# Second feed forward of a two-block transformer: three pairs of gate and up chunks as seven block products, weight blocks summed by accumulating DMA

## The chip, the cores and the metric

The kernel is one program on one core of one Trainium2 chip. The metric is device microseconds (us) of one execution. TensorE is called PE, VectorE DVE, ScalarE ACT, GpSimd POOL and SyncE SP, as in the profile.

## What is computed

The reference runs two transformer blocks on 256 tokens of width 1024, the second on the output of the first, all in float32. What matters here is the end of the second block, its gated feed forward, with a hidden width of 2816:

```python
x = x + merged @ w_out[layer]
h = rmsnorm(x, norm_ffn[layer])
x = x + (jax.nn.silu(h @ w_gate[layer]) * (h @ w_up[layer])) @ w_down[layer]
return rmsnorm(x, norm_final)
```

`w_gate` and `w_up` are 1024 x 2816, `w_down` is 2816 x 1024.

## The kernel before

Each product keeps float32 accuracy by splitting both operands in a high half, which the PE's reduced float32 format holds, and a low rest: x is held as `AH` and `AL`, a weight block as `WH` and `WL`, and a product is three matmuls, high x high, high x low and low x high (`part`, lines 441, 442 and 443). The stationary operand is a 128 x 128 block of the activation, the moving one up to 512 columns of the weights, and the result accumulates in a bank of PSUM, 128 tokens by 512 columns.

**The ring of weights.** `weight_units` lists all weight blocks in the order of use, as units of 1 MB, 128 partitions by 2048 floats. In the feed forward they go round six slots of SBUF (2, 3, 0, 1, 4, 5). `W32` of a slot receives the load; `WL` of the same slot overwrites it in place, and `WH` has its own memory. SP issues the loads in this order (`load`, line 316) and before each waits until PE is done with the unit that had the slot before; so a unit is loaded at the earliest when the sixth unit before it has been used up. ACT then writes `WH`, a copy in the reduced format, in two halves (`hi()`, line 1071), and DVE writes `WL` = `W32` - `WH`, in two halves (`lo()`, line 1579). Each engine's program is an order written out by hand, and each engine takes its instructions strictly in that order.

**The feed forward.** The hidden width is cut in 11 chunks of 256. A chunk c has two units of gate and up columns (256 and 256 columns side by side, four k tiles each) and one unit of `w_down` (two k tiles by 1024). `up2(c, tb)` multiplies one block of 128 tokens (tb is 0 or 1) by both units: 24 matmuls of 512 columns into bank 4 + tb, gate in the left half, up in the right. ACT takes silu of the gate half (`silu_gate`, line 1511), DVE multiplies it by the up half (`gated`) into `hid`, PE turns `hid` with transposes against the identity into bank 6 or 7 (`hid_turn`, line 758; the banks alternate, and a bank is free again when DVE has written the low half `HL` from it), ACT and DVE split what was turned in `HH` and `HL`, and `down2(c, tb)` multiplies by the down unit into banks 0 to 3, which hold the sum over all chunks. On PE a middle chunk is: `up2(c, 0)`, `up2(c, 1)`, `down2(c - 1, 0)`, `down2(c - 1, 1)`, and the two turns of chunk c. That is 48 + 24 matmuls of 512 columns and 4 transposes. On DVE it is `lo()`, `gated`, `lo()`, `gated`, `lo()` and two `HL`.

Besides its small reciprocal square roots (line 343) POOL has nothing to do in this part.

## Time and profile before

| | us |
|---|---|
| median of 3 runs (lowest to highest) | 726.88 (726.67 to 726.91) |
| the profiled execution | 726.56 |
| its span, first to last instruction | 724.7 |
| PE, DVE, ACT, POOL busy in the span | 715.0, 516.7, 410.6, 25.9 |

The profiled execution took 1.9 us more than its span; the median of the three runs is 0.3 us above it. In rows of the trace, "x" is a count; "idle before" is the time in which an engine had nothing to run, with what ended it; PE's own matmul time overlaps (a matmul is shown for 0.39 us where the next one starts after 0.23), so that starts, not durations, tell its rate. PEclk is the granted clock of TensorE as a share of full speed, the DMA share is the mean busy share of the core's 16 DMA engines.

### The profile page before, as it was taken

How to read it: one execution, taken by the hardware profiler on the slowest of the kernel's cores; microseconds unless marked ns; L12 is line 12 of the kernel's file. 1: busy time of each engine (PE TensorE's matmuls, PEld its weight loads, DVE VectorE, ACT ScalarE, POOL GpSimd, SP SyncE). 2: the span in 40 equal slices, each digit the busy share in tenths (PEclk: the TensorE clock that was granted, in tenths of full speed). 3: DMA queues.
4: the chain of work that ended last, by engine and by line, in shares of the span. 5: the costliest groups of instructions: out<-in, count | busy, mean ns of one | idle time of the engine just before them, and what ended most of it. 6: DMA issues, size and time to landing. Idle time of an engine off the chain costs nothing.

```text
span 724.7 us, 9660 instructions
## 1 busy us (share of the span) xinstructions
PE 715.0 (99%) x3746; PEld 572.5 (79%) x3746; DVE 516.7 (71%) x911; ACT 410.6 (57%) x691; POOL 25.9 (4%) x43
## 2 busy tenths in 40 slices
PE   8999999999999999999999999999999999999996
PEld 4678885588888888888888777778888888888885
DVE  4789999898666867847898799766856555455544
ACT  3487658985845564456556676675465443344432
POOL 1030012001000000000100000000000000000000
PEclk9999999999999999999999999999999999999999
DMA  9996939517656576643558334443366556555511
GB/s 363 415 370 229 387 104 356 204 59 261 225 180 230 203 264 242 224 175 115 162 202 291 117 119 148 151 165 121 115 229 232 178 196 202 179 175 175 175 58 59
DMA packets 72989, 145.94 MB, mean 201 GB/s; under 512 B 4128, under 2 KB 27680, under 8 KB 71920
## 3 DMA queue, kind: packets, MB, share of 16 engines
q1 hardware_dynamic: 71136, 140.03, 55.1%
q0 software_dynamic: 1520, 5.03, 2.0%
q8 instruction: 30, 0.49, 0.3%
q10 hardware_dynamic: 288, 0.27, 0.1%
q14 instruction: 15, 0.12, 0.0%
HBM read 144.27 MB, written 1.05 MB: 201 GB/s over the span
## 4 chain that ended last, share of the span: by engine, by line
PE 95%; issue 2%; DVE 1%; ACT 1%; POOL 0%; POOLq 0%; DVEq 0%
PE bank L441 23%; PE bank L443 23%; PE bank L442 23%; PE bank L786 5%; PE bank L423 5%; PE bank L784 3%; PE bank L460 1%; PE bank L515 1%; PE bank L523 1%; PE bank L518 1%; PE bank L918 1%; PE bank L940 1%; PE bank L624 1%; PE bank L500 1%; PE bank L646 1%
## 5 line engine op out<-in xcount | busy, mean ns | idle before, releaser
L1579 DVE TENSOR_TENSOR WL<-W,WH 128x1024 fp32r<-128x1024 f32 (+2 forms) x222 | 249.7, 1169 | 35.4 <-ACT WH L1071 35.3
L1071 ACT ACTIVATE WH<-W 128x1024 fp32r<-128x1024 f32 (+2 forms) x222 | 211.9, 1011 | 49.7 <-DMA W<-in_w_mlp 35.8
L441 PE MATMUL bank<-WH,AHL 128*128 128x512 f32 (+1 forms) x480 | 188.8, 393 | 0.0
L443 PE MATMUL bank<-WH,AHL 128*128 128x512 f32 (+1 forms) x480 | 185.3, 386 | 0.0
L442 PE MATMUL bank<-WL,AHL 128*128 128x512 f32 (+1 forms) x480 | 185.2, 386 | 0.0
L441 PEld LDWEIGHTS bank<-WH,AHL 128*128 128x128 f32 x480 | 90.2, 188 | 20.4 <-issue 3.2
L443 PEld LDWEIGHTS bank<-WH,AHL 128*128 128x128 f32 x480 | 90.2, 188 | 18.7
L442 PEld LDWEIGHTS bank<-WL,AHL 128*128 128x128 f32 x480 | 90.3, 188 | 17.0
L441 PE MATMUL bank<-WH,HH 128*128 128x512 f32 (+1 forms) x218 | 84.9, 390 | 0.0
L443 PE MATMUL bank<-WH,HL 128*128 128x512 f32 (+1 forms) x218 | 84.5, 388 | 0.0
L442 PE MATMUL bank<-WL,HH 128*128 128x512 f32 (+1 forms) x218 | 84.4, 387 | 0.0
L786 PE MATMUL bank<-AHL,WH 128*128 128x512 f32 x168 | 60.5, 398 | 0.0
L784 PE MATMUL bank<-AHL,WL 128*128 128x256 f32 x192 | 50.0, 281 | 0.0
L443 PEld LDWEIGHTS bank<-WH,HL 128*128 128x128 f32 x218 | 40.9, 188 | 8.5
L442 PEld LDWEIGHTS bank<-WL,HH 128*128 128x128 f32 x218 | 41.0, 188 | 8.3
L441 PEld LDWEIGHTS bank<-WH,HH 128*128 128x128 f32 x218 | 40.9, 188 | 8.0
L1511 ACT ACTIVATE rel<-bank 128x256 f32<-128x256 f32 x22 | 8.5, 384 | 62.2 <-PE bank L443 61.1
L1588 DVE TENSOR_TENSOR hid<-bank,rel 128x256 f32<-128x256 f32 x22 | 9.3, 424 | 42.2 <-ACT rel L1511 42.2
L784 PEld LDWEIGHTS bank<-AHL,WL 128*128 128x128 f32 x192 | 36.3, 189 | 2.0
L786 PEld LDWEIGHTS bank<-AHL,WH 128*128 128x128 f32 x168 | 31.6, 188 | 6.7
L1594 DVE SCALAR_TENSOR_TENSOR cacc<-hp,vec,cacc 128x256 f32<-128x256 f32 x88 | 36.0, 478 | 0.2
L1914 DVE TENSOR_TENSOR HL<-bank,HH 128x256 fp32r<-128x256 f32 (+1 forms) x26 | 11.1, 461 | 30.9 <-ACT HH L1079 30.9
(287 smaller groups left out, 852.1 us busy)
## 6 DMA issues: line engine op xcount, KB each, us to landing
W<-in_w_mlp SPq DMA_DIRECT2D x32, 1024.0 KB, 5.4
W<-in_w_in SPq DMA_DIRECT2D x24, 1024.0 KB, 5.0
W<-in_w_gate SPq DMA_DIRECT2D x22, 512.0 KB, 4.0
W<-in_w_up SPq DMA_DIRECT2D x22, 512.0 KB, 5.2
W<-in_w_down SPq DMA_DIRECT2D x11, 1024.0 KB, 4.9
W<-in_w_ada SPq DMA_DIRECT2D x10, 1024.0 KB, 8.6
WX<-in_w_ada SPq DMA_DIRECT2D x10, 1024.0 KB, 10.4
W<-in_w_out SPq DMA_DIRECT2D x8, 1024.0 KB, 5.3
```

Of the source, the lines that this page charges most:

```text
L423: ins = e.transpose(bank[b][:, c * 128:c * 128 + 128], src, m.ident[:, :])
L441: e.matmul(po, hs, wh[:, k, c0:c0 + cw], start=first and k == 0, stop=False)
L442: e.matmul(po, hs, wl[:, k, c0:c0 + cw], start=False, stop=False)
L443: ins = e.matmul(po, ls, wh[:, k, c0:c0 + cw], start=False, stop=last and k == unit.nk - 1)
L784: ins = e.matmul(bank[4 + j][:, 0:256], wl[:, k, js], m.AH[:, 4 * i + k, :], start=False, stop=False)
L786: ins = e.matmul(both, wh[:, k, js], m.AHL[:, :, 4 * i + k, :], start=False, stop=i == 1 and k == 3)
L1071: e.activation(m.WH[unit.slot][:, c], m.W32[unit.slot][:, c], ACT.Copy).then_inc(S["w_hi"], 1)
L1511: e.activation(m.rel[tb][:, 0:256], bank[bk][:, 0:256], ACT.Silu).then_inc(S["silu_g"], 1)
L1579: e.tensor_tensor(m.WL[unit.slot][:, c], m.W32[unit.slot][:, c], m.WH[unit.slot][:, c].bitcast(F32), ALU.subtract).then_inc(S["w_lo"], 1)
L1588: e.tensor_tensor(o, a, b, op).then_inc(S[sem], 1)
L1594: e.scalar_tensor_tensor(o, a, scalar, b, op0, op1).then_inc(S[sem], 1)
L1914: e.tensor_tensor(L[:, k0:k0 + nj, ts], bank[b][:, 0:nj * 128].rearrange("p (j n) -> p j n", j=nj), H[:, k0:k0 + nj, ts].bitcast(F32), ALU ...
```

## The change

Chunks 3 and 4, 5 and 6, and 7 and 8 become three groups (`PAIRS`, `GROUPS`); chunks 0, 1, 2, 9 and 10 stay as they were. The groups are numbered 0 to 7, and the pairs are groups 3, 4 and 5. For a pair, let G0, G1 be the lower and upper half of the rows of its 512 gate columns, U0, U1 those of its 512 up columns, A00, A01 the lower and upper half of the features of token block 0, and A10, A11 those of block 1. Eight products of a 128 x 512 by a 512 x 512 block would give gate and up of both token blocks. The change makes seven, each 12 matmuls (`quad_sum` and `part`):

```
0: (A10 - A11) G0            bank 4     1: (A01 - A00) U1            bank 5
2: (A00 - A11) (G0 - U1)     bank 6     3: A11 (G0 + G1)     onto bank 4
4: A00 (U0 + U1)     onto bank 5        5: (A01 - A11) (G1 + U1)     onto bank 4
6: (A10 - A00) (G0 + U0)     onto bank 5
```

Bank 4 after product 3 is the gate of block 1, bank 5 after product 4 the up of block 0; with `ysum` = product 0 + product 1 - product 2, the gate of block 0 is bank 4 + `ysum` after product 5, and the up of block 1 is bank 5 + `ysum` after product 6.

The five differences of activations (`FS`, `FH`, `FL`) are made once, ahead of chunk 2. The weights of a product are one unit of 1 MB. Those of products 0 and 1 are loaded. That of product 2 is the difference of these two, formed by DVE (`difference`, two instructions of 1024 columns) into a seventh slot. Those of products 3 to 6 are loaded by SP, and then POOL waits for that load and issues a second one of 1 MB from the other block, with `accum_op=ALU.add` (line 452 of the changed kernel), which adds to what lies in the slot; `hi()` of the unit waits for this second load. The seventh unit does not take part in the ring of six. The two down units of a pair are used together by `down2` of the pair, and a turn of a pair has four transposes instead of two. PE starts products 0 and 1 of the next group (`begin`) ahead of the pair's turns. A few semaphores are merged and renamed with no other effect.

```diff
+        self.W32.append(M("W32_6", 76, [128, 2048]))
+        self.WL.append(M("WL_6", 76, [128, 2048], F32R))
+        self.WH.append(M("WH_6", 8, [128, 2048], F32R))
...
+        self.FL = [M(f"FL{i}", (70, 72, 74, 0, 2)[i], [128, 4, 128], F32R) for i in range(5)]
+        self.ysum = M("ysum", 4, [128, 512])
+        self.g0 = M("g0", 6, [128, 512])
+        self.u0, self.u1 = self.g1b[:, 0:512], self.g1b[:, 512:1024]
...
+GROUPS = [(c, c in PAIRS) for c in range(11) if c - 1 not in PAIRS]
+NG = len(GROUPS)
+GU_ORDER = [(0, 0), (1, 0), (0, 1), (1, 1)] + [(g, tb) for g in range(2, NG) for tb in range(2)]
+HID_AT = {gt: i + 1 for i, gt in enumerate(GU_ORDER)}
...
+DN_ORDER = [(g, tb) for g in range(NG - 2) for tb in range(2)] + [(NG - 2, 0), (NG - 1, 0), (NG - 2, 1), (NG - 1, 1)]
...
+    def quad_unit(g, n, src, i, plus=None):
+        c0 = 256 * GROUPS[g][0]
+        add(("gu", g), src, 4 * i, 4, [(src, c0, 512)], True, ("gu_mm", QUAD_AT[g] + n + 1))
+        if plus:
+            w, j = plus
+            units[-1].plus = d[w][512 * j:512 * j + 512, c0:c0 + 512].rearrange("(k p) n -> p k n", p=128)
...
+    for g in range(NG + 1):
+        if g < NG and GROUPS[g][1]:
+            quad_unit(g, 0, "w_gate_2", 0)
+            quad_unit(g, 1, "w_up_2", 1)
+            first, second = units[-2:]
+            units.append(Unit(4, 512, [], True, (S["gu_mm"], QUAD_AT[g] + 3)))
+            units[-1].difference = (first, second)
+            by["gu", g].append(units[-1])
+            quad_unit(g, 3, "w_gate_2", 1, ("w_gate_2", 0))
+            down_units(g - 1)
+            quad_unit(g, 4, "w_up_2", 0, ("w_up_2", 1))
+            quad_unit(g, 5, "w_gate_2", 1, ("w_up_2", 1))
+            quad_unit(g, 6, "w_gate_2", 0, ("w_up_2", 0))
+            continue
...
-    while len(slots) < len(units):
-        slots.append((2, 3, 0, 1, 4, 5)[(len(slots) - 38) % 6])
+    ring = itertools.cycle((2, 3, 0, 1, 4, 5))
+    for unit in units[38:]:
+        slots.append(6 if unit.difference else next(ring))
...
+        if unit.plus is not None:
+            unit.base = unit.landed
+            n = sum(1 for other in units[:units.index(unit)] if other.plus is not None)
+            unit.landing_plus = S[f"l_s{n % 4}"]
+            unit.landed = (unit.landing_plus, 32 + 16 * (n // 4 + 1))
...
+    for unit in units:
+        if unit.plus is not None:
+            w.wait_ge(unit.base[0], unit.base[1])
+            e.dma_start(unit.block(m), unit.plus, accum_op=ALU.add).then_inc(unit.landing_plus, 16)
...
+    def hid_turn2(g, tb):
+        if GROUPS[g][1]:
+            turns["n"] = 1
+        hid_turn(g, 4 if GROUPS[g][1] else 2, tb, ("hid2", HID_AT[g, tb], 16 + 2 * g + tb + 1))
...
+    def begin(g):
+        if GROUPS[g][1]:
+            quad_sum(g, 0, 0, 4, True)
+            quad_sum(g, 1, 1, 5, True)
+        else:
+            up2(g, 0)
...
+    def rest(g):
...
+        quad_sum(g, 2, 2, 6, True)
+        frees(6, ("quad", 4 * q + 2))
+        w.wait_ge(S["quad_act"], 2 * q + 1)
+        part(by["gu", g][3], m.AH, m.AL, 4, 1, 4, False, True, "gu_mm", n_ready(2, 1), onto=True)
+        for tb in range(2):
+            down2(g - 1, tb, False, False)
+        w.wait_ge(S["quad"], 4 * q + 1)
+        part(by["gu", g][4], m.AH, m.AL, 0, 0, 5, False, True, "gu_mm", n_ready(2, 0), onto=True)
+        w.wait_ge(S["silu"], SILU_AT[g, 1])
+        quad_sum(g, 5, 3, 4, False)
+        frees(4, ("quad", 4 * q + 3))
+        w.wait_ge(S["quad_act"], 2 * q + 2)
+        quad_sum(g, 6, 4, 5, False)
+        frees(5, ("quad", 4 * q + 4))
 
     up2(0, 0)
...
+        rest(g)
+        if GROUPS[g][1]:
+            begin(g + 1)
+            hid_turn2(g, 0)
+            hid_turn2(g, 1)
+        else:
+            hid_turn2(g, 0)
+            hid_turn2(g, 1)
+            if g < NG - 2:
+                begin(g + 1)
+    up2(NG - 1, 0)
...
+    def quad_group(g):
+        q = quads.index(g)
+        lo(1 + GROUPS[g - 1][1])
+        w.wait_ge(S["gu_mm"], QUAD_AT[g] + 2)
+        w.wait_ge(S["quad_act"], 2 * q + 1)
+        tt(m.ysum[:, :], bank[5][:, :], m.ysum[:, :], ALU.add, "quad")
+        w.wait_ge(S["gu_mm"], QUAD_AT[g] + 3)
+        w.wait_ge(S["quad"], 4 * q + 1)
+        tt(m.ysum[:, :], bank[6][:, :], m.ysum[:, :], ALU.subtract, "quad")
+        lo(3)
+        if GROUPS[g + 1][1]:
+            difference(g + 1)
+        lo()
+        w.wait_ge(S["gu_mm"], QUAD_AT[g] + 6)
+        w.wait_ge(S["quad"], 4 * q + 2)
+        if q:
+            w.wait_ge(S["silu"], SILU_AT[quads[q - 1], 0])
+        tt(m.g0[:, :], bank[4][:, :], m.ysum[:, :], ALU.add, "quad")
+        lo()
+        w.wait_ge(S["gu_mm"], QUAD_AT[g] + 7)
+        tt(m.u1, bank[5][:, :], m.ysum[:, :], ALU.add, "quad")
+        w.wait_ge(S["hid_turned"], 4 + 2 * (g - 2) + 2)
+        w.wait_ge(S["silu"], SILU_AT[g, 0])
+        w.wait_ge(S["quad_act"], 2 * q + 2)
+        tt(m.hid[g % 2][:, 0, :], m.u0, m.rel[0][:, :], ALU.mult, "hid2")
+        w.wait_ge(S["quad"], 4 * q + 4)
+        tt(m.hid[g % 2][:, 1, :], m.u1, m.rel[1][:, :], ALU.mult, "hid2")
+        lo(2)
 
     norm_features(5, 1, m.ffn, None)
     gated(0, 0)
...
```

Where a group's turns stand on PE: the end of a chunk's down product, the turns of both token blocks, and the next chunk's first product, before. `HH0`, `HL0` are the turned hidden values of an even chunk, `hid1` those to be turned.

```order
L441 MATMUL bank3<-WH_4_65,HH0_166 128x512
L442 MATMUL bank3<-WL_4_59,HH0_166 128x512
L443 MATMUL bank3<-WH_4_65,HL0_168 128x512
L423 MATMUL bank7<-ident_80,hid1_165 128x128 x2
L423 MATMUL bank6<-ident_80,hid1_165 128x128 x2
L441 MATMUL bank4<-WH_5_66,AHL_96 128x512
L442 MATMUL bank4<-WL_5_60,AHL_96 128x512
L443 MATMUL bank4<-WH_5_66,AHL_96 128x512
```

The same place on PE now, the end of product 1 of the second pair, the turns of the first pair, and product 2 of the second pair:

```order
L505 MATMUL bank5<-WH_4_65,FH1_213 128x512
L506 MATMUL bank5<-WL_4_59,FH1_213 128x512
L507 MATMUL bank5<-WH_4_65,FL1_223 128x512
L487 MATMUL bank7<-ident_80,hid1_165 128x128 x8
L505 MATMUL bank6<-WH_6_211,FH2_214 128x512
L506 MATMUL bank6<-WL_6_210,FH2_214 128x512
L507 MATMUL bank6<-WH_6_211,FL2_224 128x512
```

The turns of the two token blocks used banks 7 and 6; both now use bank 7 (bank 6 is taken by product 2), and so the second one follows the `HL` instruction that reads the first.

On DVE, one chunk before, from the first `gated` of an odd chunk to its `HL`:

```order
L1588 TENSOR_TENSOR hid1_165<-bank4,rel0_170 128x256
L1579 TENSOR_TENSOR WL_2_57<-W32_2_51,WH_2_63 128x1024 x2
L1588 TENSOR_TENSOR hid1_165<-bank5,rel1_171 128x256
L1579 TENSOR_TENSOR WL_3_58<-W32_3_52,WH_3_64 128x1024 x2
L1914 TENSOR_TENSOR HL1_169<-bank7,HH1_167 128x2x128
L1914 TENSOR_TENSOR HL1_169<-bank6,HH1_167 128x2x128
```

On DVE now, from the difference for the second pair to the `HL` of the first pair:

```order
L1726 TENSOR_TENSOR W32_6_209<-W32_1_50,W32_4_53 128x1024 x2
L1717 TENSOR_TENSOR WL_1_56<-W32_1_50,WH_1_62 128x1024 x2
L1726 TENSOR_TENSOR g0_228<-bank4,ysum_227 128x512
L1717 TENSOR_TENSOR WL_4_59<-W32_4_53,WH_4_65 128x1024 x2
L1726 TENSOR_TENSOR g1b_74<-bank5,ysum_227 128x512
L1726 TENSOR_TENSOR hid1_165<-g1b_74,rel0_170 128x512
L1726 TENSOR_TENSOR hid1_165<-g1b_74,rel1_171 128x512
L1717 TENSOR_TENSOR WL_6_210<-W32_6_209,WH_6_211 128x1024 x2
L1717 TENSOR_TENSOR WL_5_60<-W32_5_54,WH_5_66 128x1024 x2
L2052 TENSOR_TENSOR HL1_169<-bank7,HH1_167 128x4x128 x2
```

Between the last multiplication into `hid` and the `HL` stood one weight unit, and now there stand two, the second of them (slot 5) a unit that an accumulating load completes.

## Rows read from the trace of the kernel before

**Rows 1.** The page: span, busy shares, granted clock, chain that ended last.

```profile
span 724.7 us, 9660 instructions
PE 715.0 (99%) x3746; PEld 572.5 (79%) x3746; DVE 516.7 (71%) x911; ACT 410.6 (57%) x691; POOL 25.9 (4%) x43
PEclk9999999999999999999999999999999999999999
PE 95%; issue 2%; DVE 1%; ACT 1%; POOL 0%; POOLq 0%; DVEq 0%
```

**Rows 2.** Windows: one chunk, the feed forward's middle, the end; columns in the first line.

```profile
core 0: us, PE busy (x) PEld busy (x) DVE busy (x) ACT busy (x) POOL busy (x), PEclk, DMA share, GB/s
603.79:620.59 16.80, 16.80 (x77) 13.91 (x77) 8.70 (x11) 7.11 (x10) 0.00 (x0) 1.00 0.58 187
540.00:700.00 160.00, 160.00 (x730) 132.40 (x729) 87.93 (x104) 71.82 (x104) 0.00 (x0) 1.00 0.54 178
700.00:725.00 25.00, 18.79 (x91) 15.51 (x89) 8.75 (x19) 5.34 (x15) 1.08 (x2) 0.94 0.12 43
```

**Rows 3.** Timeline of PE in one chunk: start us, length us.

```profile
602.92 0.39 PE L441 MATMUL bank<-WH,AHL 128*128 128x512 f32 x1
...
604.28 0.39 PE L441 MATMUL bank<-WH,AHL 128*128 128x512 f32 x1
...
611.77 0.60 PE L423 MATMUL bank<-ident,hid 128*128 128x128 f32 x4
612.12 0.48 PE L441 MATMUL bank<-WH,AHL 128*128 128x512 f32 x1
```

**Rows 4.** Timeline of the issues of SP's loads over one chunk.

```profile
603.79 0.37 SPq L316 DMA_DIRECT2D W<-in_w_gate  x1
...
606.51 0.37 SPq L316 DMA_DIRECT2D W<-in_w_gate  x1
...
611.96 0.37 SPq L316 DMA_DIRECT2D W<-in_w_down  x1
620.59 0.37 SPq L316 DMA_DIRECT2D W<-in_w_gate  x1
```

**Rows 5.** Windows with the DMA engines full: 2 KB, 1 KB and 4 KB rows.

```profile
231.00:235.00 4.00, 4.00 (x25) 3.51 (x24) 0.11 (x1) 1.20 (x2) 0.00 (x0) 1.00 1.04 395
606.50:611.00 4.50, 4.50 (x21) 3.72 (x21) 2.79 (x3) 2.28 (x3) 0.00 (x0) 1.00 1.08 360
614.00:616.00 2.00, 2.00 (x10) 1.65 (x10) 2.00 (x2) 0.80 (x1) 0.00 (x0) 1.00 1.02 422
```

**Rows 6.** DMA issues by line: size of each, median us from issue to landing.

```profile
W<-in_w_mlp SPq DMA_DIRECT2D x32, 1024.0 KB, 5.4
...
W<-in_w_down SPq DMA_DIRECT2D x11, 1024.0 KB, 4.9
...
g1b<-in_final_g POOLq DMA_DIRECT2D x1, 512.0 KB, 4.3
```

**Rows 7.** Groups by form of the last 185 us: busy us, mean ns, idle before.

```profile
L1579 DVE TENSOR_TENSOR WL<-W,WH 128x1024 fp32r<-128x1024 f32 x60 | 70.7, 1222 | 14.0 <-ACT WH L1071 14.0
L1071 ACT ACTIVATE WH<-W 128x1024 fp32r<-128x1024 f32 x58 | 58.1, 1054 | 0.1
L1588 DVE TENSOR_TENSOR X<-bank,X 128x512 f32<-128x512 f32 x4 | 2.8, 692 | 3.7 <-PE bank L443 3.7
L1083 ACT ACTIVATE S<-X 128x512 f32<-128x512 f32 x3 | 1.9, 632 | 6.7 <-DVE X L1588 6.7
```

**Rows 8.** Timeline of DVE and ACT: a weight unit's two halves back to back.

```profile
607.89 2.36 DVE L1579 TENSOR_TENSOR WL<-W,WH 128x1024 fp32r<-128x1024 f32 x2 [0.52 <-ACT WH L1071]
606.80 2.00 ACT L1071 ACTIVATE WH<-W 128x1024 fp32r<-128x1024 f32 x2
```

More of the change, by code:

```diff
@@ L187, in __init__ @@
         self.nk, self.wid, self.pieces, self.split, self.free = nk, wid, pieces, split, free
+        self.plus = self.difference = None
     def block(self, m):
@@ L288, in weight_units @@
             last[p] = unit
+        if unit.difference:
+            unit.landed = (S["diff"], 2 * sum(1 for other in units[:units.index(unit) + 1] if other.difference))
+            continue
         landed[slot] = landed.get(slot, 0) + 16 * len(unit.pieces)
@@ L311, in load @@
         unit = units[n]
+        if unit.difference:
+            return
         for old in unit.old:
@@ L425, in turn, with part @@
         return b
-    def part(unit, H, L, k0, tb, bk, first, last, sem, ready, c0=0, cw=512):
+    def part(unit, H, L, k0, tb, bk, first, last, sem, ready, c0=0, cw=512, onto=False):
         wh = m.WH[unit.slot][:, 0:unit.nk * unit.wid].rearrange("p (k n) -> p k n", k=unit.nk)
@@ L440, in part @@
             ls = L[:, k0 + k, tb * 128:tb * 128 + 128]
-            e.matmul(po, hs, wh[:, k, c0:c0 + cw], start=first and k == 0, stop=False)
-            e.matmul(po, hs, wl[:, k, c0:c0 + cw], start=False, stop=False)
-            ins = e.matmul(po, ls, wh[:, k, c0:c0 + cw], start=False, stop=last and k == unit.nk - 1)
+            e.matmul(po, hs, wh[:, k, c0:c0 + cw], start=first and k == 0, stop=False, skip_group_check=onto)
+            e.matmul(po, hs, wl[:, k, c0:c0 + cw], start=False, stop=False, skip_group_check=onto)
+            ins = e.matmul(po, ls, wh[:, k, c0:c0 + cw], start=False, stop=last and k == unit.nk - 1, skip_group_check=onto)
         ins.then_inc(S[sem], 1)
@@ L1018, in down2 @@
+    def down2(g, tb, first, last, ns=(0, 1)):
         for n in ns:
-            unit = by["dn", c][0]
-            part(unit, m.HH[c % 2], m.HL[c % 2], 0, tb, 2 * n + tb, first, last, "dn_mm",
-                 lambda k: ("hid_lo", 16 + 2 * c + tb + 1), 512 * n, 512)
+            for i, unit in enumerate(by["dn", g]):
+                part(unit, m.HH[g % 2], m.HL[g % 2], 2 * i, tb, 2 * n + tb, first and i == 0, last, "dn_mm",
+                     lambda k: ("hid_lo", 16 + 2 * g + tb + 1), 512 * n, 512)
@@ L1112, in scalar_program @@
     w.wait_ge(S["l_cs"], 16)
-    e.activation(m.cs[:, :], m.cs[:, :], ACT.Silu).then_inc(S["silu_c"], 1)
+    e.activation(m.cs[:, :], m.cs[:, :], ACT.Silu).then_inc(S["silu"], 1)
     for tb in range(2):
@@ L1530, in scalar_program @@
         hid_hi2(1, tb)
-    for c in range(2, 10):
-        hi()
-        silu_gate(c, 0)
-        hi()
-        silu_gate(c, 1)
-        hi()
+    for i in range(5):
+        form_hi(i)
+    for g in range(2, NG - 1):
+        if GROUPS[g][1]:
+            quad_group(g)
+        else:
+            hi()
+            silu_gate(g, 0)
+            hi()
+            silu_gate(g, 1)
+            hi(2 if GROUPS[g + 1][1] else 1)
         for tb in range(2):
-            hid_hi2(c, tb)
+            hid_hi2(g, tb)
     hi()
-    silu_gate(10, 0)
-    hid_hi2(10, 0)
+    silu_gate(NG - 1, 0)
+    hid_hi2(NG - 1, 0)
     def last_squares(tb):
@@ L2272, in vector_program, with gated @@
     lo()
-    def gated(c, tb, bk=None):
+    quads = [g for g in range(NG) if GROUPS[g][1]]
+    def gated(g, tb, bk=None):
         bk = 4 + tb if bk is None else bk
-        w.wait_ge(S["silu_g"], GU_AT[c, tb] // 2)
-        if c > 1:
-            w.wait_ge(S["hid_turned"], 4 + 2 * (c - 2) + tb + 1)
-        tt(m.hid[c % 2][:, tb, 0:256], bank[bk][:, 256:512], m.rel[tb][:, 0:256], ALU.mult, "hid2")
-    def hid_lo2(c, tb):
-        hid_lo(c, 2, tb, 16 + 2 * c + tb + 1)
+        w.wait_ge(S["silu"], SILU_AT[g, tb])
+        if g > 1:
+            w.wait_ge(S["hid_turned"], 4 + 2 * (g - 2) + tb + 1)
+        tt(m.hid[g % 2][:, tb, 0:256], bank[bk][:, 256:512], m.rel[tb][:, 0:256], ALU.mult, "hid2")
@@ new lines, in difference, with quad_group @@
+    def difference(g):
+        unit = by["gu", g][2]
+        for old in unit.old:
+            w.wait_ge(old.free[0], old.free[1])
+        for source in unit.difference:
+            w.wait_ge(source.landed[0], source.landed[1])
+        for p in range(2):
+            c = slice(1024 * p, 1024 * p + 1024)
+            x, y = (m.W32[source.slot][:, c] for source in unit.difference)
+            tt(m.W32[unit.slot][:, c], x, y, ALU.subtract, "diff")
+    def quad_group(g):
+        q = quads.index(g)
+        lo(1 + GROUPS[g - 1][1])
[11 more added lines that the diff above has]
+        w.wait_ge(S["quad"], 4 * q + 2)
+        if q:
+            w.wait_ge(S["silu"], SILU_AT[quads[q - 1], 0])
[10 more added lines that the diff above has]
+        lo(2)
```

225 lines of the change are left out of this document (140 added, 85 removed).

## Prediction

> **What bounds the kernel now.** I read the page first [rows 1]: PE is busy 715.0 of 724.7 us, the chain that ended last is 95% PE, and the granted clock is full in every slice. Then the windows [rows 2]: in one chunk of the feed forward PE is busy 16.80 of 16.80 us, while DVE works 8.70, ACT 7.11, and the DMA engines are busy 58% of the time; from 540 to 700 us the picture is the same. So PE alone sets the time here and only fewer matmuls shorten it, but each of the three others has a known distance to PE, and the change moves all three. The timeline of PE gives the unit of account [rows 3]: from 602.92 to 604.28 six matmuls started, 0.227 us each. 72 of them are 16.3 us of the chunk's 16.80 (the period of the issues in [rows 4]); the other 0.5 us is the four transposes.
>
> **What PE saves.** Seven products of 12 matmuls replace eight: 12 fewer per pair, 36 in all, which is also what the two programs' rows differ by (2490 against 2526 of 512 columns; the transposes stay the same in number). 36 x 0.227 = 8.2 us. The Trainium skill (TensorE: Matmul & The Clock Gate, "Wait — 56ns, not 53.3ns?") gives 215.7 ns as the start to start time of 512 columns; by it the gain would be 7.8 us. The trace's 227 ns is what I use. A pair then needs 84 + 48 matmuls and 8 transposes: 132 x 0.227 + 1.0 = 30.9 us of PE, where two chunks needed 33.6.
>
> **What DVE and ACT get.** A weight unit costs DVE 2.36 us and ACT 2.00 us [rows 8] (each half 1.22 and 1.05 us by itself, [rows 7]). Two chunks have 6 units, a pair in the middle has 7 + 2 = 9. DVE: 9 x 2.36 = 21.2, the difference of two units 2.4 (the same shape), and eight instructions of 512 columns (two into `ysum`, g0, u1, two `hid`, two `HL`) at 0.69 [rows 7], 5.5: together 29.1 us against 17.4 before (2 x 8.70, [rows 2]). That is 94% of PE's 30.9. ACT: 9 x 2.00 + six of 0.63 = 21.8 us. Totals fit, so neither costs anything by its sum; what costs is DVE's order. The forming of the five activation differences (5 + 5 instructions of 0.69 us on DVE, 5 of 0.63 on ACT, before chunk 2) lies in chunks where DVE has 8.1 us free of 16.8 [rows 2], and what follows it on DVE, the `HL` of chunk 1, isn't wanted by PE until 48 matmuls later; nothing.
>
> **The wait that the turns add.** Both turns of a pair use bank 7, and the second may start only when DVE's `HL` has read the first. After PE's product 6 DVE has u1, two `hid` (3 x 0.69), two weight units (4.7) and `HL` (0.69): 7.5 us, plus 0.3 us by which DVE comes late, since between the ends of products 5 and 6 (2.7 us) stand g0 and a unit (3.05 us). PE has in that time 24 matmuls of the next group and the first four transposes, 5.4 + 0.5 = 5.9 us. PE waits about 2 us in each pair, three times: 6 us. Everything behind the second turn on PE waits too, product 2 and 3 of the next group and the down product. The bounds are 3 us (DVE never late) and 11 us (DVE late by a unit and a half, as the difference ahead of it makes possible). This alone takes most of the 8.2 us.
>
> **What the DMA engines get.** Before, a chunk loads 3 MB in 16.8 us. With the engines full, the trace shows 395 GB/s for rows of 2 KB and 422 for rows of 4 KB [rows 5], so 2.65 us for a gate or up unit of a pair (its rows are 2 KB) and 2.5 for a down unit. A pair in the middle needs six loads of 2 KB rows and two down units, 20.9 us, and four accumulating loads of 1 MB. The trace has no accumulating load. Its lower bound is the plain load, 2.65 us: the same bytes come from memory. It can't be below that. But an addition into the slot has to fetch what lies there as well: two MB read for one written. If reading is what fills an engine, it takes 5.3 us. I take 5.3, since nothing in the kernel shows an engine reading faster than it writes, and 2.65 as the other end; nothing in the trace bounds it above.
>
> Then the sum over the three pairs. Let T0 be the start of product 0 of the first pair. By the ring of six, the units of products 0, 1, 3 and 4 have been requested before T0 (the last of these 5.9 us before, when chunk 2's second unit is used up: 606.51 against the period's 603.79 and 620.59 in [rows 4] gives the place), that of product 5 is requested 0.9 us before, that of 6 at T0 + 2.7. So at T0 there are left 18 plain loads (2 of this pair, 8 of each of the next two, four of them down units) and 11 accumulating ones. PE needs the last one at the start of product 6 of the last pair: 25.4 (first pair, with one down unit) + 30.9 + 27.2 (six products and the down products) = 83.5 us after T0, and the load has to be down some 3 us before (landing, one half by ACT, one by DVE), 80.4. DMA work: 14 x 2.65 + 4 x 2.5 + 11 x 2.65 = 76 us at the lower end, which just fits; at 5.3 it is 47 + 58 = 105 us, 25 us too much. Loads hardly run ahead of that, since SP may fill a slot only when PE is done with the sixth unit before it: **the ring holds no stock for the DMA engines to work off.**
>
> To this comes time in which the engines stand idle although they are the bound. A load takes 5.4 us to land where 1 MB is 2.65 us of work, and a POOL load of half that size 4.3 us [rows 6]: about 3 us of each are not transfer. An accumulating load begins only when POOL has seen the first one landed, 12 times; most of these 36 us lie beside other loads. I charge a sixth, 6 us; the bounds are 0 and 12. The Trainium skill (DMA: Bandwidth & Descriptors, "Issuing engines are not separate DMA queues") says that loads issued from different engines run on the same 16 DMA engines; by that rule POOL's loads bring no bandwidth of their own, and the sum above would stand.
>
> **The sum.** 25 (DMA) + 6 (idle) + 2 (turn wait of the last pair, where no load can hide it; in the others the DMA wait covers it) - 8.2 = +25 us. The profiled execution took 726.6, so 751.5; from the median 726.9 it is 751.9. I predict 752. Its own range is 740 (an accumulating load at 4.3 us) to 765 (12 us idle and PE at a lower clock after its longest waits: at the end of the kernel, where PE idles 6.2 of 25 us, the granted clock is 0.94 [rows 2], that is 3 us at half speed).
>
> **The rivals.**
> (a) An accumulating load costs no more than a plain one. The DMA work then fits (76 of 80 us), PE waits for the turns and, in the first pair, for a chain of load, addition and split that is too long (0 to 6, I take 3). Of the turns I take 9 here rather than 6, since nothing but DVE's queue then sets them and in two pairs the difference (2.4 us) stands in it ahead of g0: 9 + 3 - 8.2 = +4, so 731, from 725 (turns 6, chain 0) to 736 (11 and 6). For it: the bytes from memory are the same. The Trainium skill (same page, "Where 436 GB/s comes from") puts the ceiling at 435 GB/s; at that rate 29 MB would take 70 us, and by it this rival would stand; the trace's full windows show 360 to 422 [rows 5].
> (b) The other side, faster: the additions are hidden as in (a), and DVE's queue runs far enough ahead that the second turn finds bank 7 free. It decides at one point: whether `HL` of the first turn comes within 5.9 us of product 6's end. By instruction counts it comes after 7.5; two units of 2.36 us would have to be done earlier, which their place in DVE's order excludes unless product 6 itself is late. Then 36 matmuls less 1 or 2 us of waits: 720, from 718 to 725.
> (c) An accumulating load costs far more than two plain ones, 8 us: 47 + 88 = 135 us, 55 too much, and PE at the lower clock between: about 782.
> (d) The change doesn't do what it says. The programs' rows exclude it: 36 matmuls are gone.
>
> **How the numbers follow.** Forecast 0.5, (a) 0.28, (b) 0.08, (c) 0.12, the rest 0.02. The range is to hold 8 in 10: from 728, inside (a), to 772, which leaves out (b), the lowest part of (a) and (c). Within 0.2% (1.45 us, about what a measurement of this kernel can tell from no change) lies only a strip of (a): 0.05. Faster: (b) and a little of (a), 0.09. Slower 0.86.
>
> **What would show it.** In the profile after: 36 fewer matmuls of 512 columns; the start to start time still 0.227 us. In the windows of the pairs, the DMA share near 1 for some 80 to 110 us where it was 0.55, and PE busy well below its window; the first weight halves on ACT (`WH`) waiting for a DMA, DVE for ACT, PE for `WL`. The landing of POOL's accumulating loads: 8 us or more from issue supports 5.3 us of work, 5 to 6 us supports (a). PE idle about 2 us before a transpose of line 487, released by `HL`, in all three pairs. It would be wrong if the DMA share stays below 0.9 and the landings short (then (a)), or if no transpose waits (then the step on DVE's order fails), or if ACT never waits for a load in the pairs.

## The result, and the profile after

The changed kernel takes 757.5 us (median of 4 runs, 754.6 to 759.1) where the kernel before took 726.8 (4 runs, 726.6 to 726.9): 1.0418 times as long, 95% interval 1.0381 to 1.0456, or 30.7 us more. The profiled execution took 754.6 us, 28.0 more than that of before.

The page of the changed kernel, the lines that answer to [rows 1], and that on the DMA engines:

```profile
span 752.6 us, 9651 instructions
PE 715.1 (95%) x3710; PEld 569.6 (76%) x3710; DVE 554.5 (74%) x945; ACT 433.4 (58%) x708; POOL 41.3 (5%) x55
...
PEclk9999999999999999999999999999999979989999
DMA  8995949424675676465384334433578999999611
```

PE has 36 matmuls fewer and is busy just as long (715.0 before). Both can hold only if the remaining ones ran more slowly, and the clock line says where: at the end of the kernel, in the slices where the DMA line stands at 9. (The page's chain that ended last covers only 17% of the span here, so the readings below go by windows and timelines.)

Windows of the changed kernel: from the issue of product 3's unit to the third pair, from the start of product 0 of the first pair to the start of product 6 of the last (answers to the second line of [rows 2]), and one stretch in which PE worked at the lower clock:

```profile
core 0: us, PE busy (x) PEld busy (x) DVE busy (x) ACT busy (x) POOL busy (x), PEclk, DMA share, GB/s
561.71:690.00 128.29, 104.37 (x432) 83.11 (x431) 82.35 (x88) 60.71 (x75) 15.32 (x12) 0.92 1.04 278
578.68:695.45 116.77, 92.85 (x379) 73.55 (x378) 69.50 (x70) 53.50 (x63) 13.97 (x11) 0.91 1.07 289
604.00:610.00 6.00, 4.99 (x12) 3.80 (x12) 2.00 (x2) 0.55 (x1) 0.00 (x0) 0.50 1.09 264
```

The DMA share was 0.54 in this part and is now above 1 (the times of packets overlap) for more than 128 us, but with 278 GB/s where full engines gave 395 before [rows 5].

Waits of PE in the part with the pairs: us in total, times, longest. In it PE waited for nothing before, apart from the kernel's end:

```profile
PE bank L487 <- DVE HL L2052: 11.6, 3, 6.0
PE bank L505 <- DVE WL L1717: 6.8, 2, 5.0
PE bank L505 <- ACT g1b L1187: 5.0, 2, 2.8
PE bank L505 <- DVE g L1726: 3.2, 2, 1.7
```

26.6 us in all. The first line is the second turn of each pair, the second the weights of products 4 and 5 of the first pair, the third product 6, which needs bank 5 copied by ACT and its weights, and the fourth the next group's product 0, which needs bank 4 read by `g0`.

PE's timeline, the first pair: the start of product 0, the end of product 4, product 5, the start of product 6, the start of the next group's product 0, and the two turns. Answers to [rows 3]:

```profile
578.68 0.48 PE L505 MATMUL bank<-WH,FH 128*128 128x512 f32 x1
...
599.41 0.39 PE L506 MATMUL bank<-WL,AHL 128*128 128x512 f32 x1
599.64 0.39 PE L507 MATMUL bank<-WH,AHL 128*128 128x512 f32 x1
605.01 0.77 PE L505 MATMUL bank<-WH,FH 128*128 128x512 f32 x1 [4.98 <-DVE WL L1717]
605.58 0.63 PE L506 MATMUL bank<-WL,FH 128*128 128x512 f32 x1
...
613.17 0.52 PE L505 MATMUL bank<-WH,FH 128*128 128x512 f32 x1 [2.81 <-ACT g1b L1187]
...
619.28 0.50 PE L505 MATMUL bank<-WH,FH 128*128 128x512 f32 x1 [1.50 <-DVE g L1726]
...
625.00 0.60 PE L487 MATMUL bank<-ident,hid 128*128 128x128 f32 x4
628.58 0.63 PE L487 MATMUL bank<-ident,hid 128*128 128x128 f32 x4 [2.98 <-DVE HL L2052]
```

Up to 599.64 the starts are 0.227 us apart, as before. After a wait of 4.98 us they are 0.42 to 0.43 apart: the granted clock is 0.50 (1.2 of 2.4 GHz) from 604 to 610, and product 5, 12 matmuls, costs 5 us in place of 2.7. The wait is paid, and then the work behind it takes nearly twice its time.

What the weights did meanwhile, ACT's timeline (the first of each pair of halves of `WH` waits for a load to land):

```profile
594.60 2.00 ACT L1179 ACTIVATE WH<-W 128x1024 fp32r<-128x1024 f32 x2 [10.39 <-DMA W<-in_w_up]
...
602.55 2.00 ACT L1179 ACTIVATE WH<-W 128x1024 fp32r<-128x1024 f32 x2 [5.47 <-DMA W<-in_w_up]
610.63 2.00 ACT L1179 ACTIVATE WH<-W 128x1024 fp32r<-128x1024 f32 x2 [6.08 <-DMA W<-in_w_up]
```

and POOL's issues of the same three accumulating loads (products 4, 5 and 6):

```profile
582.16 1.29 POOL L452 DMA_DIRECT2D W<-in_w_up  x1 [13.76 <-DMA W<-in_w_up]
...
587.48 1.26 POOL L452 DMA_DIRECT2D W<-in_w_up  x1 [1.44 <-DMA W<-in_w_gate]
```

They were issued 2.7 us apart (the middle one at 584.77) and land 8.0 apart, the last 23 us after its issue. Of the DMA issues of 560 to 720 us one line answers to [rows 6] (KB, median us to landing):

```profile
W<-in_w_up POOLq DMA_DIRECT2D x9, 1024.0 KB, 14.8
```

The instructions of DVE and ACT themselves are as long as before [rows 7]: a half of `WL` 1221 ns, of `WH` 1052, one of 512 columns on DVE 684 to 688.

One sign in the description of the change is the other way round in the kernel: DVE forms `ysum` as product 2 less products 0 and 1 (bank 6 less what `ysum` holds). With that sign bank 4 + `ysum` is the gate of block 0 and bank 5 + `ysum` the up of block 1. The number of instructions and their times stay the same.

### The profile page after: what moved, and what is told of

It is laid out like the page before. It is cut to its first block and busy times, and to the rows that moved or that the text cites. A ratio compares the mean times of both kernels' runs of the same rounds, so it can differ in the third digit from the quotient of the medians.

```text
span 752.6 us, 9651 instructions
## 1 busy us (share of the span) xinstructions
PE 715.1 (95%) x3710; PEld 569.6 (76%) x3710; DVE 554.5 (74%) x945; ACT 433.4 (58%) x708; POOL 41.3 (5%) x55
## 5 line engine op out<-in xcount | busy, mean ns | idle before, releaser
L1717 DVE TENSOR_TENSOR WL<-W,WH 128x1024 fp32r<-128x1024 f32 (+2 forms) x240 | 270.5, 1173 | 68.8 <-ACT WH L1179 68.4
L1179 ACT ACTIVATE WH<-W 128x1024 fp32r<-128x1024 f32 (+2 forms) x240 | 229.5, 1014 | 103.9 <-DMA W<-in_w_up 45.5
L505 PE MATMUL bank<-WH,AHL 128*128 128x512 f32 (+1 forms) x408 | 160.5, 393 | 2.0 <-DVE WL L1717 2.0
L507 PE MATMUL bank<-WH,AHL 128*128 128x512 f32 (+1 forms) x408 | 157.3, 385 | 0.0
L506 PE MATMUL bank<-WL,AHL 128*128 128x512 f32 (+1 forms) x408 | 157.1, 385 | 0.0
L505 PEld LDWEIGHTS bank<-WH,AHL 128*128 128x128 f32 x408 | 76.7, 188 | 20.6 <-issue 5.4
L507 PEld LDWEIGHTS bank<-WH,AHL 128*128 128x128 f32 x408 | 76.7, 188 | 15.8
L506 PEld LDWEIGHTS bank<-WL,AHL 128*128 128x128 f32 x408 | 76.7, 188 | 14.2
L505 PE MATMUL bank<-WH,FH 128*128 128x512 f32 x60 | 26.9, 449 | 13.2 <-ACT g1b L1187 5.0
L401 POOL TENSOR_TENSOR stat<-stat 128x1 f32<-128x1 f32 x12 | 10.1, 848 | 492.1 <-DVE stat L1741 446.0
L1187 ACT ACTIVATE HH<-bank 128x512 fp32r<-128x512 f32 (+1 forms) x20 | 9.3, 487 | 31.6 <-PE bank L487 31.6
## 6 DMA issues: line engine op xcount, KB each, us to landing
W<-in_w_up POOLq DMA_DIRECT2D x9, 1024.0 KB, 14.8
```

The source lines that it names most:

```text
L401: e.tensor_tensor(m.stat[:, 40 + i:41 + i], m.stat[:, 24 + i:25 + i], m.stat[:, 94:95], ALU.pow).then_inc(S["rstd"], 1)
L505: e.matmul(po, hs, wh[:, k, c0:c0 + cw], start=first and k == 0, stop=False, skip_group_check=onto)
L506: e.matmul(po, hs, wl[:, k, c0:c0 + cw], start=False, stop=False, skip_group_check=onto)
L507: ins = e.matmul(po, ls, wh[:, k, c0:c0 + cw], start=False, stop=last and k == unit.nk - 1, skip_group_check=onto)
L1179: e.activation(m.WH[unit.slot][:, c], m.W32[unit.slot][:, c], ACT.Copy).then_inc(S["w_hi"], 1)
L1187: e.activation(o, i, ACT.Copy, scale=scale).then_inc(S[sem], 1)
```

## Experiments: which part costs what

Each kernel was timed in the same session as the kernel before (medians 726.65 to 726.78); "waits" are the lines of PE's waits as above, summed; "`HL` early" and "SP held" are told below; and "clock" is worked out from windows of 1 us of each trace, from 540 us on, as the sum of PE's busy time x (1 - granted clock). "Sum" is waits + clock - 0.227 us for each matmul saved; it should come near to the profiled run less 726.6. The rows with a plain second load or none leave the sums of weights out; they show times, not usable kernels.

| | median us | ratio (95%) | waits | clock | sum | profiled run - 726.6 |
|---|---|---|---|---|---|---|
| the change | 757.5 | 1.0418 (1.0381 to 1.0456) | 26.6 | 7.4 | 25.8 | 28.0 |
| second load plain | 742.3 | 1.0214 (1.0198 to 1.0229) | 18.9 | 3.4 | 14.1 | 15.7 |
| no second load | 732.6 | 1.0079 (1.0064 to 1.0094) | 9.2 | 5.0 | 6.0 | 6.6 |
| no second load, `HL` early | 725.05 | 0.9979 (0.9969 to 0.9988) | 5.7 | 0.0 | -2.5 | -1.7 |
| the change, `HL` early | 755.45 | 1.0399 (1.0382 to 1.0417) | 27.1 | 6.7 | 25.6 | 28.7 |
| one pair | 740.3 | 1.0187 (1.0172 to 1.0202) | 10.3 | 4.6 | 12.2 | 13.3 |
| one pair, `HL` early | 737.1 | 1.0141 (1.0126 to 1.0156) | 8.8 | 2.6 | 8.7 | 9.7 |
| two pairs apart, `HL` early | 750.3 | 1.0327 (1.0312 to 1.0343) | 20.1 | 5.9 | 20.6 | 23.4 |
| one pair, SP held to product 5 | 733.0 | 1.0083 (1.0068 to 1.0098) | 6.3 | 1.6 | 5.2 | 6.7 |
| one pair, SP held to product 6 | 737.5 | 1.0144 (1.0129 to 1.0159) | 8.7 | 4.2 | 10.2 | 11.2 |
| three pairs, SP held to product 5 | 749.8 | 1.0318 (1.0300 to 1.0335) | 20.1 | 6.3 | 18.2 | 22.6 |

The sum finds all but 0.6 to 4.4 us each time. Much of this rest lies in how a wait is counted: it starts at the shown end of the matmul before it, 0.39 us after that one's start, where without a wait the next would have started after 0.227. Each wait so leaves out 0.16 us (0.25 behind a group of transposes). For the nine waits of the change this makes 2.1 of 2.2 us, for the thirteen of the last row 2.4 of 4.4. What is left, up to 2.0 us, I haven't traced.

### The addition taken out of the second load

```diff
-            e.dma_start(unit.block(m), unit.plus, accum_op=ALU.add).then_inc(unit.landing_plus, 16)
+            e.dma_start(unit.block(m), unit.plus).then_inc(unit.landing_plus, 16)
```

> The changed kernel, with the second load of products 3 to 6 left as it is in size, place, queue and waits, but plain: it overwrites the slot instead of adding to it, so the sums of weights are left out. Theory 1 (the addition doubles the load's work on the DMA engines): the DMA work after T0 falls from 105 to 76 us and fits, what is left are the turn waits and the first pair's chain, so 727 to 738 us. Theory 2 (the chain load, POOL, second load is what costs): 750 or more, as the changed kernel's 757. Theory 3 (DVE's order alone): no change from 757.

742.3 us: the addition alone, with the same bytes from memory, in the same places and behind the same waits, costs 15.2 us of the 30.7. But 15.6 us are left without it, and the time is 4 us above the upper end of the 727 to 738 that I expected.

### No second load at all

```diff
-            unit.landed = (unit.landing_plus, 32 + 16 * (n // 4 + 1))
...
-    for unit in units:
-        if unit.plus is not None:
-            w.wait_ge(unit.base[0], unit.base[1])
-            e.dma_start(unit.block(m), unit.plus, accum_op=ALU.add).then_inc(unit.landing_plus, 16)
```

> The changed kernel without the second load of products 3 to 6 (the sums of weights are left out, the split waits for the first load only). Theory 1: all DMA waits are gone, and the price of the turns stands alone: 726.8 - 8.2 + 9 to 12, so 728 to 731 us. Theory 2: the same, and a good deal less than with the plain second load. If the turn waits are hidden once loads are early (my rival b): 719 to 722.

732.6 us. The second loads, even plain, cost 9.7 us. And with no load to wait for the change is still 5.9 us slower than the kernel before of the same session, 1.6 us above what I expected at most. PE's waits are then

```profile
PE bank L482 <- DVE HL L2047: 8.2, 3, 2.9
PE bank L500 <- DVE g L1721: 1.0, 1, 1.0
```

and the windows after the first turn show the clock:

```profile
610.00:612.00 2.00, 0.19 (x2) 0.22 (x3) 1.66 (x2) 0.00 (x0) 0.00 (x0) 1.00 1.02 370
612.00:616.00 4.00, 4.00 (x14) 3.22 (x13) 2.00 (x3) 3.37 (x5) 0.00 (x0) 0.57 0.36 137
```

A wait of 2.61 us, to 611.81, is followed by 4 us at 0.57 of full clock, so the turn costs 2.6 + 4 x 0.43 = 4.3 us.

### No second load, and `HL` ahead of the last weight unit

```diff
         tt(m.hid[g % 2][:, 1, :], m.u1, m.rel[1][:, :], ALU.mult, "hid2")
-        lo(2)
+        for tb in range(2):
+            lo()
+            hid_lo2(g, tb)
```

and the same on ACT with `hi()` and `hid_hi2`, for the chunk before a pair too.

> As the run without the second load (the sums of weights are left out), and with the HL of a pair's two turns moved up on DVE, and HH on ACT: one weight unit, HL of the first turn, one weight unit, HL of the second, where both weight units stood ahead. If the wait of a pair's second turn is due to DVE's order, each of the three falls from about 3 to about 1 us: 6 us less than without the second load, so 722 to 725. If the wait is due to something else (DVE's total, bank 7 as such), no change.

725.05 us, 7.5 less than without the move, and 1.6 less (0.2%) than the kernel before: the only one of these kernels that is faster. It leaves the 12 additions out, so it is no version to use; it is the best of the orders that were run, with nothing loaded twice. What remains of the turn wait is 1.56 us in each pair, after which no window shows a lower clock:

```profile
PE bank L482 <- DVE HL L2049: 4.7, 3, 1.6
```

By the table the two profiled runs lie 8.3 us apart, 3.5 of it waits and 5.0 clock that doesn't fall any more.

### The whole change with `HL` early

> The changed kernel whole, with the two HL of a pair moved up between the two weight units on DVE (and HH on ACT). Without the second loads this order took 7.5 us off. Theory 1 (with them the DMA engines are the bound of the three pairs): what the turns give back is spent waiting for weights, except in the last pair; 752 to 756 us, 2 to 5 less than the changed kernel's 757.5. If the waits add up independently: 750.

755.45 us, where the change took 754.6 to 759.1: no difference that the runs can tell. The turn waits fell from 11.6 to 4.7 us, and the waits for product 6 (5.0 before) and for `WL` (6.8, now 7.8) rose by as much:

```profile
PE bank L505 <- ACT g1b L1187: 11.3, 3, 4.4
...
PE bank L487 <- DVE HL L2054: 4.7, 3, 1.6
```

The same edit is worth 7.5 us without the second loads and nothing beside them: the turn lies under the wait for loads.

### The price of an accumulating load by itself

The kernel before, with loads of 1 MB (2 KB rows) behind its end, first single ones, then four plain and four accumulating in a row:

```diff
...
+            if add:
+                e.dma_start(dst, src, accum_op=ALU.add).then_inc(S[f"l_b{n % 4}"], 16)
+            else:
+                e.dma_start(dst, src).then_inc(S[f"l_b{n % 4}"], 16)
...
```

> The kernel before, and after its last output has landed POOL issues loads of 1 MB (2 KB rows of w_up_2) with nothing else running: one plain, one accumulating, again one plain, one accumulating, then four plain back to back, then four accumulating back to back, each step waiting for the one before. Nothing of the output changes; the kernel is longer by this tail. Theory 1 (an accumulating load keeps the DMA engines busy about twice as long as a plain one): the four plain take about 10.6 us plus 3 of latency, the four accumulating about 21 plus 3, at about 200 GB/s. Theory 2 (the addition costs no bandwidth, what hurts in the pairs is that the second load is issued by POOL after the first one's landing): both fours take about 11 to 14 us. Theory 3 (far dearer than twice): over 30 us for the four.

Windows inside the four plain and the four accumulating loads:

```profile
757.00:761.00 4.00, 0.00 (x0) 0.00 (x0) 0.00 (x0) 0.00 (x0) 0.34 (x1) 0.50 1.01 394
771.00:788.00 17.00, 0.00 (x0) 0.00 (x0) 0.00 (x0) 0.00 (x0) 2.82 (x3) 0.50 1.10 198
```

and POOL's issues; each waits for the landing of the one ahead:

```profile
725.22 0.80 POOL L400 DMA_DIRECT2D W<-in_w_up  x1 [3.88 <-DMA out<-S]
731.11 1.32 POOL L398 DMA_DIRECT2D W<-in_w_up  x1 [5.09 <-DMA W<-in_w_up]
739.91 0.77 POOL L400 DMA_DIRECT2D W<-in_w_up  x1 [7.47 <-DMA W<-in_w_up]
```

198 GB/s against 394, with the engines full both times: 1.0486 MB take 5.3 us accumulating and 2.66 plain (expectations written after this run put the first at 5.1). A single one lands 8.8 us after its issue began, a plain one 5.9. With these rows of 2 KB an accumulating load costs two plain ones.

## Experiments: the order in which the engines serve

### One pair alone

```diff
-PAIRS = (3,5,7)
+PAIRS = (3,)
```

> The changed kernel with one pair (chunks 3 and 4) instead of three. Theory 1: at the pair's start 2 plain and 3 accumulating loads are left, 5.3 + 15.4 = 20.7 us of DMA work (5.1 us per accumulating load as measured alone) for about 18.8 us, so 2 us late; with a turn wait of 3, some 1.5 us of lowered clock, less 2.7 of matmuls: +4, 730 us. A per-pair cost that is the same for each pair (a third of 30.7 us) would give 737.

740.3: the first pair alone costs 13.6 of the 30.7 us, where I expected 3 to 4. By the sum over whole stretches a single pair, with chunks before and behind it that leave 42% of the DMA engines free, should have found its bandwidth. So the sum of work over whole stretches isn't what decides in the first pair.

### One pair, and two pairs apart, with `HL` early

> One pair, with the HL moved up. Theory 1: 2 to 2.5 us less than one pair without, 727 to 728 us: about even with the kernel before. It beats the kernel before only if the DMA work of the one pair is hidden entirely (725).

> Two pairs that do not follow each other (chunks 3 and 4, 7 and 8, two ordinary chunks between), HL moved up. Between the pairs the ordinary chunks use 58% of the DMA engines, so theory 1 lets the second pair start as the first did: twice the single pair's difference to the kernel before, 727 to 731 us. If the accumulating loads of both pairs queue up all the same: 735 or more.

737.1 and 750.3 (`PAIRS = (3, 7)`), both above what I expected: 10.4 us for one, 23.7 for two, and 28.8 for three in a row. In the run with two apart, PE's waits from 672 to 730 us, those of the second pair, repeat those of the first (4.9, 1.5 and 1.6 us):

```profile
PE bank L505 <- DVE WL L1719: 4.8, 2, 3.8
PE bank L505 <- ACT g1b L1187: 2.4, 1, 2.4
PE bank L487 <- DVE HL L2054: 1.6, 1, 1.6
```

A pair behind a single chunk pays each time; with three in a row 7.3 of the 7.8 us of `WL` waits stand in the first pair. Between product 3 and 4 a pair behind a pair has 48 matmuls of the down product on PE, a pair behind a single chunk 24, which is 5.4 us less cover for the first two late units. That this is the reason is my reading; no run changed it alone.

### Both kinds of load at the same time

The kernel before again, with four plain loads from POOL behind its end, then four accumulating ones and, beside these, eight plain loads from SP.

> The kernel before, with a part behind it that computes nothing of the reference: four plain loads of 1 MB from POOL, then four accumulating loads of 1 MB from POOL to the same places, and beside these eight plain loads of 1 MB (2 KB rows) that SP issues one behind the other. Measured alone before: plain 2.7 us per MB, accumulating 5.1. Theory 1, the DMA engines serve both streams byte for byte: while both run, an accumulating load lands every 5.1 + 2.7 = 7.8 us, and so does a plain one; the first four of SP's are down when the four of POOL are, after some 31 us, and the other four follow at 2.7. Theory 2, the engines give both streams equal time: an accumulating load every 10.2 us, a plain one every 5.4. Theory 3, the accumulating loads go first: one every 5.1 us, the plain ones afterwards. Theory 4, the plain ones go first: eight in 22 us, and no accumulating load lands before. In all four the whole work is 42 us.

The window of 743 to 774 us, with both kinds in flight, and its queues (q0 is POOL's, q1 SP's; packets, MB, share):

```profile
743.00:774.00 31.00, 0.00 (x0) 0.00 (x0) 0.00 (x0) 0.00 (x0) 1.70 (x2) 0.50 1.09 267
```

```profile
q0 software_dynamic: 1905, 3.80, 66.0%
q1 hardware_dynamic: 2257, 4.47, 43.0%
```

In 31 us 3.80 MB accumulated and 4.47 MB plain: one load of 1.0486 MB every 8.6 and every 7.3 us. That is theory 1 (7.8 and 7.8) and not 2 (10.2 and 5.4): the streams share nearly byte for byte, so that each plain load in flight adds its own time to an accumulating one. Neither queue goes first. In the changed kernel the same stands in ACT's rows: 8.0 us from one landing to the next, 5.3 + 2.7. The Trainium skill (DMA: Bandwidth & Descriptors, "Issuing engines are not separate DMA queues") says that DMAs of all issuing engines run on the same 16 engines and interleave; this run agrees, with 267 GB/s in common.

### SP's loads held back

The one change that takes the sharing away without taking work away: SP's first load behind the unit of product 6, and with it all behind it, waits for an accumulating load of that pair to have landed.

```diff
+    for g in range(NG):
+        if GROUPS[g][1]:
+            units[units.index(by["gu", g][6]) + 1].after = by["gu", g][5]
...
+        if unit.after is not None:
+            w.wait_ge(unit.after.landed[0], unit.after.landed[1])
```

> One pair (chunks 3 and 4), HL of the first turn ahead of the weight units, as in the run that took 737.06; and now SP's first load behind the unit of product 6 (a down unit, with all loads behind it) waits until the accumulating load of product 5 has landed. Theory of the shared engines: in the run without this wait SP's plain loads for the next group took every other MB from POOL's accumulating loads, and each of products 4 to 6 waited 2.7 us more than its load needs. With the wait the accumulating loads land 5.1 us apart and the kernel takes 730 to 733. Theory of the whole work: the bytes are the same and only their order changes; nothing is won, 737, or more, up to 740, since plain loads now start late.

> The same one pair, but SP's loads behind the unit of product 6 wait until the accumulating load of product 6 has landed. Theory of the shared engines: products 4, 5 and 6 all get their weights at 5.1 us per load, but the DMA engines serve plain loads 5 us later than with the wait on product 5, and the next chunk starts with less stock: 730 to 735. Theory of the whole work: 737 to 742.

> Three pairs, HL early, as in the run that took 755.45, and SP's loads behind each pair's unit of product 6 wait until the accumulating load of product 5 has landed. Theory of the shared engines: the first pair gains 4 to 5 us as the single pair does, but with pairs in a row the DMA engines have no free time between them, so the next pairs win little or nothing: 750 to 752. Theory of the whole work: the engines are full in any order, 755; and if the wait leaves them idle for a landing time of 2 to 3 us in each pair, 757 to 763.

One pair: 733.0 with the wait on product 5's load, 4.0 us less than without it (737.1, 1.0141 against 1.0083 times the kernel before, intervals apart). ACT's rows show why:

```profile
593.37 2.01 ACT L1184 ACTIVATE WH<-W 128x1024 fp32r<-128x1024 f32 x2 [8.70 <-DMA W<-in_w_up]
...
598.43 2.00 ACT L1184 ACTIVATE WH<-W 128x1024 fp32r<-128x1024 f32 x2 [2.57 <-DMA W<-in_w_up]
603.92 2.00 ACT L1184 ACTIVATE WH<-W 128x1024 fp32r<-128x1024 f32 x2 [3.48 <-DMA W<-in_w_up]
```

5.1 and 5.5 us apart, where the same kernel without the wait had 6.9 and 6.8. In this kernel the first load of product 4, asked for before product 0, lands 3.4 us after product 0's start (582.57 against 579.14), and product 6's weights land 24.8 us after that start. Three accumulating and two plain loads are 21.2 us of work, so with the 3.4 us the engines do little else than what the pair needs. The balance of the prediction counted product 4's first load as done at that point; in the changed kernel it wasn't either (POOL's row at 582.16, 3.5 us after 578.68).

Held until product 6's load has landed, the kernel takes 737.5, as much as without a wait and not the 730 to 735 that I expected from shared engines. The time alone would fit the other theory, but the rows show both effects: the three landings are early (5.1 and 5.0 us apart), the next chunk's are late, and PE waits 4.2 us for `g0`, which stands on DVE behind the weight units. Three pairs: 749.8, 5.6 us less, with the intervals apart (1.0300 to 1.0335, and 1.0382 to 1.0417). Its waits are 7.0 us shorter, 3.2 of them in the first pair, but as much again in the third, where I had expected little or nothing. It moves the same bytes. So a part of the loss was order and not volume, and it can be had by holding back a load that nobody needs yet. No kernel with its additions comes below the kernel before; the nearest, one pair with SP held to product 5, is 0.8% slower.

## Why the prediction was right, and where not

I predicted 752 us, from 728 to 772, and 757.5 was measured: slower, with the DMA engines full and the turns waiting, as forecast. That the sum came within 5.6 us is in good part luck, since two of its terms were off by more than that, one up and one down, and the main term was right in size but not in where it falls. By its steps:

**What PE saves** held: 36 matmuls, still 0.227 us from start to start at full clock.

**What the DMA engines get**: the price held. 5.3 us were taken from "two MB read for one written", and 5.3 were measured alone. The time from T0 to the last pair's product 6, 83.5 + 25 + 6 = 114.5 in my sum, was 116.8 (578.68 to 695.45). This agreement too is partly luck: of the 33.3 us over 83.5, 15.0 are waits for the products' weights and banks, but 9.0 are waits at two turns (the longer one late by a load too, see below) and 7.4 are lower clock, which those 31 us did not hold. The experiments split it otherwise as well. Taken away one behind the other, the additions gave 15.2 us and the second loads 9.7: 24.9, where I had charged 25 + 6. The extra 6 were for idle engines, and that step failed in kind: the DMA share is 1.07 over the whole stretch, so they were not idle but busy with loads that were not wanted yet. Holding these back won 5.6 us with the same bytes. The balance over the whole stretch, with a deficit spread over three pairs, is also what made me expect 730 for a single pair, which took 740.3. Of these 10 us the sharing with loads for later took 4.0 (with `HL` early); product 4's first load held the engines for 3.4 us that the balance left out; and the clock cost 4.6 where I had some 1.5. In the trace the waits for weights stand at the front (6.8 us for `WL`, all in the first pair), and from 672 to 700 us, in the third pair, PE waits for no load at all. Part of that is cover by the turns before it: with `HL` early PE waits 4.3 us there, for product 6 and a `WL`.

**The wait that the turns add**: the mechanism held, the size didn't. I had 2 us for each pair, from 7.5 us of DVE's work behind product 6 and "0.3 us by which DVE comes late". DVE's timeline at the first pair:

```profile
611.72 2.36 DVE L1717 TENSOR_TENSOR WL<-W,WH 128x1024 fp32r<-128x1024 f32 x2 [5.72 <-ACT WH L1179]
614.00 2.35 DVE L1726 TENSOR_TENSOR W<-W,W 128x1024 f32<-128x1024 f32 x2
616.27 2.35 DVE L1717 TENSOR_TENSOR WL<-W,WH 128x1024 fp32r<-128x1024 f32 x2
618.54 0.68 DVE L1726 TENSOR_TENSOR g<-bank,ysum 128x512 f32<-128x512 f32 x1
...
621.41 0.68 DVE L1726 TENSOR_TENSOR g1b<-bank,ysum 128x512 f32<-128x512 f32 x1
...
623.21 4.62 DVE L1717 TENSOR_TENSOR WL<-W,WH 128x1024 fp32r<-128x1024 f32 x4
627.75 0.68 DVE L2052 TENSOR_TENSOR HL<-bank,HH 128x512 fp32r<-128x512 f32 x1
```

From 611.72, when the last accumulating load was through ACT, DVE works without a gap to the end of `HL` at 628.43. Product 6's last matmul started at 617.38, but u1 (`g1b`) begins only at 621.41: DVE is some 3.5 us late, not 0.3, because the late load pushed a unit, the difference for the next pair and another unit in front of `g0` and u1. In the second pair the unit ahead of `HL` itself waits for a load:

```profile
667.46 2.00 ACT L1179 ACTIVATE WH<-W 128x1024 fp32r<-128x1024 f32 x2 [5.65 <-DMA W<-in_w_gate]
```

and the turn waits 6.0 us. The three waits are 3.0, 6.0 and 2.6. What I said of their cover held: with the additions in, moving `HL` wins nothing that the runs can tell.

**The clock** is the term that the sum lacked. I had it in the range's upper end only, as 3 us after the longest waits. It is 7.4 us in the change and 5.0 where nothing but turns waits. Without second loads the changes on PE and DVE cost 14.1 us against the 8.2 saved (732.6 - 726.7 + 8.2): 9.2 of waits, 8.2 of them at the turns, for which rival (a) had 9, and 5.0 of clock. The sum had 2 for them. So two terms were off, against each other: 6 too much for the engines, 12 too little for turns and clock; together they leave 6, about the 5.6 us between 751.9 and 757.5.

**The rivals.** The run with plain second loads is the world of (a): I gave it 731, at most 736, and it took 742.3, with 18.9 us of waits for my 12, and 3.4 of clock. Had the additions been free, the time would have been inside my range but (a)'s own sum 11 us short. At the 394 GB/s that full engines showed with 2 KB rows its 29 loads take 77 us, not 70, which just fits its 80. (b) needed the second turn to find bank 7 free; it didn't even with `HL` moved up and no load to wait for, and the best time seen is 725.05, above (b)'s 720 and at the edge of its range. (c) is excluded by 5.3 us per load.

**What would show it**: the share stands near 1 from 561 to 705 us, longer than the 80 to 110 that I wrote; the landings are 14.8 us (8 or more); ACT waits 42.1 us for the loads of `in_w_up`, DVE for ACT, PE for `WL`; a turn waits in all three pairs. DVE's busy time grew by 37.8 us and ACT's by 22.8; my counts gave 42 and 26. The forming of the activation differences is the ten instructions on DVE and five on ACT that I had taken, so the excess lies in how I priced some rows, which I haven't split further. That term carried nothing.

Open are the up to 2.0 us that waits, their counting and the clock don't explain, and why the pairs of a row cost less than those apart, beyond the reading given there. The split of the loss in parts also depends on the order in which they are taken away, as the edit of `HL` shows.

## What to carry to other kernels

A saving on the bound engine is worth what the others can follow: here 8.2 us of matmuls were worth 1.6 us at best before any extra byte was moved, because one bank and DVE's order put a wait of 1.6 to 3 us into each pair. Price a DMA that accumulates as two loads, and then look at which loads are in flight beside it: prefetches that nobody waits for take turns with it. Where waits enter a PE stream that had none, the work at half clock behind them belongs in the sum and not only in the range: here it was 7.4 us beside 26.6 of waits, and 5.0 beside 9.2.
